# Modulation products of 512 columns in four column tiles, and a first layer that is modulated after its transpose

## What is computed

```python
h = rms_norm(x, g) * (1 + scale) + shift      # shift, scale, gate: rows of silu(cond) @ ada_w + ada_b
# cond = c_ctx for the 128 context tokens, c for the 256 latent tokens
aq, ak, av, bq, bk, bv, bo, bg = split(h @ ab_w_in)      # layer 0: attention and mLSTM
... mixers ...; x = x + gate * mixed; then a mixture of 32 experts; the same for layer 1
```

## Time and profile before

| | us |
|---|---|
| median of 3 runs | 1768.45 |
| lowest and highest | 1767.39, 1774.14 |
| span of the profiled execution | 1768.3 |
| TensorE busy | 1582.3 (89%) |
| VectorE busy | 427.1 (24%) |
| ScalarE busy | 301.4 (17%) |
| first product of TensorE | 16.8 |
| first product of the input projection | 58.7 |
| end of the last modulation chunk of the projection's rounds | 197.3 |

### The profile page before, as it was taken

How to read it: one execution, slowest core, us unless ns; L and a number is a source line. 1 busy time by engine, 2 the same in 40 slices (tenths; PEclk the granted TensorE clock), 3 DMA queues, 4 the chain that set the end, 5 groups by cost and what they waited for, 6 DMA issues and landing times.

```text
span 1768.3 us, 21532 instructions
## 1 busy us (share of the span) xinstructions
PE 1582.3 (89%) x8498; PEld 781.0 (44%) x8498; DVE 427.1 (24%) x911; ACT 301.4 (17%) x606; POOL 145.3 (8%) x199
## 2 busy tenths in 40 slices
PE   4899876897999999999957998898899999999991
PEld 3454775644443333334423445654333333344440
DVE  0212275423311111111113022323411111111113
ACT  1100112411111111111112003431111111111112
POOL 1101103000000000000014000010000000000000
PEclk8899977697999999999987998998899999999996
DMA  9977944024999999999969422022499999999982
GB/s 352 256 255 258 347 179 161 1 75 166 372 423 423 424 424 423 424 423 424 423 278 303 159 95 84 1 76 113 179 419 423 424 424 423 423 424 424 423 372 110
DMA packets 99382, 522.15 MB, mean 295 GB/s; under 512 B 10090, under 2 KB 11562, under 8 KB 56320
## 3 DMA queue, kind: packets, MB, share of 16 engines
q1 hardware_dynamic: 85920, 485.58, 68.1%
q0 software_dynamic: 13408, 35.81, 6.4%
HBM read 511.60 MB, written 20.22 MB: 301 GB/s over the span
## 4 chain that ended last, share of the span: by engine, by line
PE 82%; DVE 6%; DMA 6%; ACT 3%; issue 2%; SPq 1%; POOL 0%; DVEq 0%; POOLq 0%; ACTq 0%
PE psum L827 24%; PE psum L517 14%; PE psum L840 12%; PE psum L808 9%; PE psum L773 5%; DMA ring<-in_moe_w 3%; PE psum L833 2%; PE psum L814 2%; PE psum L820 2%; PE psum L460 2%; PE psum L726 2%; PE psum L688 1%; PE psum L706 1%; ACT area_g L1091 1%; DMA ring<-in_ada_w 1%
## 5 line engine op out<-in xcount | busy, mean ns | idle before, releaser
L827 PE MATMUL psum<-ring,area_t 128*64 128x512 f32 x1024 | 450.1, 592 | 3.5 <-DMA ring<-in_moe_w 1.4
L828 PE MATMUL psum<-ring,area_t 128*64 128x512 f32 x1024 | 450.4, 593 | 0.0
L827 PEld LDWEIGHTS psum<-ring,area_t 128*64 128x64 f32 x1024 | 139.3, 137 | 292.8 <-issue 291.3
L517 PE MATMUL psum<-ring,area_t 128*128 128x512 f32 (+1 forms) x576 | 241.6, 581 | 0.0
L840 PE MATMUL psum<-ring,area_t 128*64 128x512 f32 x1024 | 235.5, 602 | 2.2 <-DVE area_t L1676 2.2
L808 PE MATMUL psum<-area_h,area_t 128*64 128x512 f32 x768 | 180.0, 604 | 3.0 <-DVE area_t L1661 3.0
L1647 DVE COPY area_q<-psum 64x512 f32<-64x512 f32 x64 | 44.5, 695 | 570.6 <-PE psum L828 570.5
L517 PEld LDWEIGHTS psum<-ring,area_t 128*128 128x128 f32 x576 | 110.0, 192 | 127.6 <-issue 125.8
L1853 POOL DMA_INDIRECT pair_rows<-area_q,idx x64 | 62.3, 973 | 940.3 <-ACT area_q L1137 925.7
L828 PEld LDWEIGHTS psum<-ring,area_t 128*64 128x64 f32 x1024 | 139.3, 137 | 0.0
L840 PEld LDWEIGHTS psum<-ring,area_t 128*64 128x64 f32 x1024 | 68.7, 137 | 120.5 <-issue 113.1
(11 more groups left out here) (238 smaller groups left out, 1363.0 us busy)
## 6 DMA issues: line engine op xcount, KB each, us to landing
ring<-in_moe_w SPq DMA_DIRECT2D x192, 2048.0 KB, 16.2
ring<-in_ada_w SPq DMA_DIRECT2D x24, 2048.0 KB, 16.9
ring<-in_na_w_in SPq DMA_DIRECT2D x6, 2048.0 KB, 18.0
ring<-in_ab_w_in SPq DMA_DIRECT2D x5, 2048.0 KB, 11.3
area_m<-mod_ready POOLq DMA_DIRECT2D x6, 1024.0 KB, 8.9
area_q<-pair_rows POOLq DMA_DIRECT2D x6, 1024.0 KB, 7.0
ring<-in_ab_w_out SPq DMA_DIRECT2D x2, 2048.0 KB, 15.6
area_g<-mod_ready POOLq DMA_DIRECT2D x4, 1024.0 KB, 7.7
```

What stands on the lines that cost most here:

```text
L517: mm = pe.matmul(banks[2 + g % 4][:, 0:w], hT[:, k, t * P:t * P + P], wchunk(n, KT)[:, k, 0:w], start=(k == 0), stop=(k == KT - 1))
L827: pe.matmul(banks[2 + u][0:64, :], lhsT, w1[:, k, :], start=(k == 0), stop=(k == KT - 1))
L828: mm = pe.matmul(banks[2 + u][64:128, :], lhsT, w3[:, k, :], start=(k == 0), stop=(k == KT - 1))
```

## The change

- A modulation chunk is 8 products with 512 columns instead of 32 with 128. Product k goes to column tile k % 4; each tile sums two k, and PSUM bank 7 holds four partial sums of one chunk. Every chunk is copied by ScalarE for itself (24 copies instead of 6), and a chunk's first product waits for the copy of the chunk before it. In DRAM `mod_raw` has a dimension of 4 for the partial sums, which VectorE adds in `modulation` (three more additions for each group).
- In the projection's rounds from the second on, one of the two modulation chunks runs after the first token tile and one after the third (`ADA_AFTER`), instead of both at the end.
- For the first layer h is no longer made row by row. `turn_first` turns x while it scales: the moving operand is a diagonal matrix with the reciprocal norm (`first_diagonal`). When a chunk has been copied, `columns` sums the partial sums and turns them into columns by four products with two columns each; VectorE adds the bias columns and the gain, and `hT` is scaled and shifted by partition, by VectorE (six operations for each half) and ScalarE (two).
- The first input chunk is loaded third instead of fifth, and projected in two halves of k: the first four k when chunks 0 and 2 (shift and scale of the first 512 features) are through, the others after chunks 1 and 3. It uses three PSUM banks at once.
- GpSimd loads 24 rows of bias and gain instead of the bias row and the repeated gain row, no longer waits for h_ready ahead of the small loads, and SyncE no longer waits for first_gain_loaded. The stores and reads of groups are put in another order: group 4 is fetched ahead of the mLSTM state stores.

```diff
+        FIRST = [(0, 0), (0, 2), (0, 1), (0, 3)]
...
-        stream = [("ada", 0, c) for c in range(4)]
+        stream = [("ada",) + q for q in FIRST[0:2]] + [("in", 0, 0)] + [("ada",) + q for q in FIRST[2:4]]
...
                 for k in range(KT):
-                    for j in range(4):
-                        mm = pe.matmul(banks[7][32 * j:32 * j + 32, 128 * (c % 4):128 * (c % 4) + 128],
-                                       cond32[:, k, :], w[:, k, 128 * j:128 * j + 128],
-                                       start=(k == 0), stop=(k == KT - 1 and not (l == 0 and c < 4)),
-                                       skip_group_check=True)
...
+                    j = k % 4
+                    mm = pe.matmul(banks[7][32 * j:32 * j + 32, :], cond32[:, k, :], w[:, k, :],
+                                   start=(k < 4), stop=(k >= 4), skip_group_check=True)
...
+            def columns(l, c):
+
+                n = ADA_NUM[l, c]
+                if n == 0:
+                    pe.wait_ge(S["first_ready"], 1)
+                pe.wait_ge(S["ada_copied"], n + 1)
+                for i in range(4):
+                    col = (c // 2) * 2 * KT + 2 * (4 * (c % 2) + i)
+                    mm = pe.matmul(banks[6][:, col:col + 2], modsb[:, n % 2, P * i:P * i + P], keep[:, KEEP["cond"]],
+                                   start=True, stop=True)
+                mm.then_inc(S["cols_done"], 1)
...
+            def project_first():
+
+                n = NUM["in", 0, 0]
+                for half in range(2):
+                    for c in (half, half + 2):
+                        ada(0, c)
+                        columns(0, c)
+                    pe.wait_ge(landed[place(n)], when(n))
+                    pe.wait_ge(S["first_scaled"], 2 * half + 2)
+                    for t in range(NT):
+                        for k in range(4 * half, 4 * half + 4):
+                            mm = pe.matmul(banks[2 + t][:, :], hT[:, k, t * P:t * P + P], wchunk(n, KT)[:, k, :],
+                                           start=(k == 0), stop=(k == KT - 1), skip_group_check=True)
+                        if half:
+                            mm.then_inc(S["proj_done"], 1)
+                ada_step(("in", 0))
...
+            def first_columns(half):
+
+                v.wait_ge(S["cols_done"], 2 * half + 2)
...
+                v.wait_ge(S["trans_copied"], 2 * NT)
+                for k in range(4 * half, 4 * half + 4):
+                    for c, cols in enumerate((slice(0, P), slice(P, 3 * P))):
+                        if c == 0 or k % 4 >= 2:
+                            ins = v.tensor_scalar(hT[:, k, cols], hT[:, k, cols], scale0[:, k, c:c + 1],
+                                                  shift0[:, k, c:c + 1], ALU.mult, ALU.add)
...
-            get(first_gain, spread(a["norm_mix"][0]), "first_gain_loaded")
...
             get(early, a["early"], "early_loaded")
 
-            pool.wait_ge(S["h_ready"], NT)
             gv = a["ab_q_norm"][0]
             get(qkgain[:, 0:A_HEADS, :], gv.unsqueeze(0).unsqueeze(0).to_broadcast([P, A_HEADS, HD]), "small_loaded")
...
+            finish_mod(4)
             pool.wait_ge(S["cstate_ready"], 2)
```

More of the change, by code:

```diff
@@ L464, in ada @@
[L464 to L471, removed]
-                mm.then_inc(S["ada_done"], 1)
@@ L474, in ada_step @@
-            def ada_step(which):
-                for q in ADA_AT[which]:
-                    ada(*q)
[L478 to L490, removed]
+                    j = k % 4
@@ new lines, in turn_first @@
+            def turn_first(t):
+                pe.wait_ge(S["h_ready"], t + 1)
+                for half in range(2):
+                    n = 2 * t + half
+                    if n >= 2:
+                        pe.wait_ge(S["trans_copied"], n - 1)
+                    for k in range(4):
+                        d0 = (4 * half + k) * P
+                        mm = pe.matmul(banks[n % 2][:, k * P:k * P + P], x[:, t, d0:d0 + P], diag[:, t, :],
+                                       start=True, stop=True)
+                    mm.then_inc(S["trans_done"], 1)
@@ L492, in transpose_rows, with ada_step @@
+            def ada_step(which, part=None):
+                for q in ADA_AT[which] if part is None else ADA_AT[which][part:part + 1]:
+                    ada(*q)
             def transpose_rows(idx, t):
@@ L1184, in _ @@
                 squares(t)
-            ada_copy(0)
-            for c in range(2):
-                act.wait_ge(S["first_spread"], c + 1)
-                step(act.copy(spread_view(modB[:, c, :]), spread_banks(c, 0)), "first_B")
+            for t in range(NT):
+                copy_transposed(0, t)
+            for half in range(2):
+                ada_copy(0, half)
+                ada_copy(0, half + 2)
+                scale_first(half)
             for l in range(2):
-                for t in range(NT):
-                    copy_transposed(2 * l, t)
+                if l:
+                    for t in range(NT):
+                        copy_transposed(2 * l, t)
                 copy_projected(l)
@@ L1254, in modulation @@
                 v.wait_ge(S["cmod_loaded"], 32 * G)
-                m = cmod[:, G % 2, :, :, :]
+                m, r = cmod[:, G % 2, :, :, :], craw[:, G % 2, :, :]
+                flat = m.rearrange("p c v i -> p (c v i)")
+                tt(flat, r[:, 0, :], r[:, 1, :], ALU.add)
+                for j in range(2, 4):
+                    tt(flat, flat, r[:, j, :], ALU.add)
                 for c in range(2):
@@ L1751, in rows @@
                         normed(idx, t - behind)
-            first_modulation()
             for t in range(NT):
-                normed(0, t)
+                first_diagonal(t)
+            v.wait_ge(S["first_rows_turned"], 1)
+            cp(first.rearrange("p v k -> p (v k)"), banks[6][:, 32:32 + 3 * KT], "first_ready")
+            for half in range(2):
+                first_columns(half)
             for l in range(2):
```

171 lines of the change are left out of this document (101 added, 70 removed).

## The result

| | us |
|---|---|
| before, median of 18 runs | 1767.06 (1763.21 to 1774.14) |
| after, median of 18 runs | 1779.29 (1764.93 to 1783.32) |
| ratio after to before | 1.0052, 95% interval 1.0035 to 1.0069 |
| span of the profiled execution, before and after | 1768.3, 1777.7 |

The change makes the kernel slower, by 0.5% or 9 us: inside the range (1753 to 1785), and 4 us worse than the +4.9 of the forecast. It lies right at the bound of 0.5% between "no change" and "slower": the interval leaves out 1, and has values on both sides of 1.005.

A forecast was written before the change was run, and what follows sets the result against it. The start was taken to be bound by weight arrival, slowed by uncovered small loads, then by TensorE. Mark +3.3, rounds +1.0, turned pair +0.9, attention -0.3 gave +4.9 on 1768.3: 1773 us, range 1753 to 1785.

The forecast's parts named there:

- What bounds the start: Kernel start: uncovered small loads slow weight streaming for 23 us to 1.88 MB, so modulation chunk 2 arrives at 41 us.
- Rival A: Small loads at the start cost only their bytes, 1.9 us: mark at 72.5, whole 1757.6 us; chance 0.20.
- first half: First four k of the first input projection: 12 products, 10.4 us plus 1.8 for low clock, from 49.0 to 61.2.
- Rival B: Modulation chunks: four tiles with long products run two at a time, 3.47 us a chunk, +35, 1808 us; chance 0.05.
- rival C: First projection: clock stays low through the broken-up start, halves 20.8 us instead of 12.2, +17, 1790 us; chance 0.07.
- The mark: End of the first projection chunk and its two modulation chunks: 88.1 us instead of 84.79, +3.3.
- open stretch: Between the projection halves: two modulation products, copies, columns and VectorE with nothing to cover them, 10.4 us.
- second half: Remaining k of the first input projection: 12.2 us, from 71.6 to 83.8, with the same clock loss of 1.8.
- pair: Two modulation chunks after the first projection, with one copy between them: 1.8 + 0.7 + 1.8 = 4.3 us.
- Rounds: Five later projection rounds, modulation chunks standing apart and switching the tiling twice: +1.0 us, bounds -1 and +3.
- turned pair: Behind the projections: second turned chunk waits for ScalarE's copy of the first, 0 to 1.8 us, taken +0.9.
- Attention: End of the mLSTM: a pair adds 0.6, earlier group fetch lets the key copy start up to 0.8 sooner; net -0.3 us.

The follow-up runs named there:

- the first attempt: Changed kernel with GpSimd's small loads made to wait until two projection chunks are done, ahead of the modulation stores in its queue: ratio 1.0151 to the kernel before.
- the second: Changed kernel with the unslimmed small loads issued after the store of modulation chunk 7, so no store waits behind them: ratio 0.9960 to the kernel before.

## Why the prediction was right, and where it was off

**What bounds the start** held. The forecast put a slow stretch of 23 us with 1.88 MB of weights behind the removed wait. After has 2.45 MB from 17 to 41 us. Chunk 2 was foreseen for 41 and came at 41.91, and the wait ahead of it was 13.05 (I had said about 20, with TensorE's work ahead of it done by about 22; transposes, chunk 1 and its columns took until 28.9). That was the one step that decided the sign. Rival A, by which the loads cost only their bytes, asked for the first half near 33. It was near that (33.1 to 37.3) only in the kernels that take the loads or their packets away. Rival B fell with chunks of 1.85 to 1.92 us at the high clock (3.64 at the low one, for chunk 2), rival C with halves of 12.48 and 13.26.

The Trainium skill ("DMA: Bandwidth & Descriptors", Queues, rings and completion order) says that engines take turns between queues packet by packet. The trace agrees: 174 packets of q0 beside 170 of q1 in 14 us. It is less even with the two gain loads alone in the kernel before, 165 beside 253 in the same 14 us. In after a packet of q0 took 1.2 us of an engine and one of q1 0.079 x 14 x 16 / 170 = 0.10, so that equal turns were no equal shares.

**The mark** was sized at +3.3 and was +6.1. Step by step, against the forecast:

| step | forecast | after | difference |
|---|---|---|---|
| chunk 2's product begins | 41.0 | 41.91 | +0.9 |
| from there to the first half | 8.0 | 8.83 | +0.8 |
| first half | 12.2 | 12.48 | +0.3 |
| open stretch | 10.4 | 9.84 | -0.6 |
| second half | 12.2 | 13.27 | +1.1 |
| pair | 4.3 | 4.57 | +0.3 |

The largest is the second half. I gave the clock's loss, 1.8 us, to both halves alike; against 10.4 at the high clock the first lost 2.1 and the second 2.9. The dense first half did leave the clock high, as I took it to, for the open stretch. The windows of after (columns as above) show where it went:

```profile
63.00:71.00 8.00, 6.03 (x49) 2.77 (x48) 0.38 (x3) 1.17 (x2) 0.00 (x0) 1.00 0.98 363
71.00:73.00 2.00, 0.00 (x0) 0.00 (x0) 1.88 (x7) 1.09 (x2) 0.00 (x0) 0.68 0.48 185
73.00:77.00 4.00, 3.94 (x5) 1.85 (x6) 0.00 (x0) 0.00 (x0) 0.00 (x0) 0.50 0.07 27
77.00:79.00 2.00, 2.00 (x4) 0.78 (x3) 0.00 (x0) 0.00 (x0) 0.00 (x0) 0.61 0.00 0
79.00:87.00 8.00, 8.00 (x26) 3.20 (x28) 1.26 (x2) 0.58 (x1) 0.00 (x0) 1.00 0.00 0
```

The granted clock was 1.00 until 71 us, fell to the lower of its two levels (1.2 GHz) while TensorE had nothing to do (from 70.5 to 73.06), stayed there in the first 4 us of dense work and was back at the upper one (2.4 GHz) before 79.

The arrival of chunk 2 is the next, 0.9. Of the 0.8 behind it, 0.5 are the four products with two columns, 1.88 us at half clock where I took 1.4 between 0.9 and 1.8: the upper bound was the value. The other 0.3 are VectorE's, 2.6 where I took 2.3.

Two sums of the forecast are slightly off, and nothing hangs on them: the upper bound of the open chain adds up to 12.7, not 12.5, and the terms given for the upper end of the range to 1786.5, not 1785.

**Rounds and turned pair.** Rounds: foreseen +1.0, measured 113.96 - 112.58 = +1.4 for the five (90.90 to 204.86, before 84.79 to 197.37). A full round has 0.26 of it: 0.07 for two chunks at 1.85 us instead of 1.815, the rest for the projection in two pieces (7.06 + 13.93 = 20.99 instead of 20.80). Turned: foreseen +0.9, measured 0.36. The first row shows the 1.67 us for the copy that I had counted. But before, TensorE waited 1.84 us for VectorE at this place, and the delay falls into that wait. In after VectorE still comes last, by 0.39:

```profile
212.38 1.92 PE L459 MATMUL psum<-ring,cond 128*32 128x512 f32 x16 [1.67 <-ACT area_m L1011]
214.69 0.39 PE L561 MATMUL psum<-small,keep 128*128 128x4 f32 x2 [0.39 <-DVE small L1265]
```

**Attention** was foreseen at -0.3; from the sums to the turned keys it was -0.65 (83.91, before 84.56), and the 6.48 us wait of VectorE is gone. The size proves little: kernels with this part of after's code unchanged took 83.7 to 86.2 us for it.

**Behind that** the sum had nothing, and the trace has +3: attention itself +0.4, from there to the first expert product +1.3, and the rest +2.6 until the last expert product and -2.1 behind it. I didn't find one cause for these. The projection of layer 1 is one part, 125.63 instead of 124.17 us. The change doesn't touch it: all 24 modulation chunks are done by 295 us. The difference goes with the clock of these two executions, in the first 7 us (before, then after):

```profile
944.93:952.00 7.07, 7.07 (x17) 3.16 (x17) 0.00 (x0) 0.58 (x1) 7.07 (x11) 0.91 1.08 311
...
955.03:962.00 6.97, 6.97 (x13) 3.00 (x13) 0.00 (x0) 0.58 (x1) 6.97 (x11) 0.70 1.07 311
```

The last group of expert products is another: 5.35 us before and 3.65 in after, 1.7 of the -2.1. Together: 6.1 + 1.7 - 0.65 + 0.4 + 1.3 + 2.6 - 2.1 = 9.4, the difference of the spans. The medians differ by 12.2, the ratio by 9.

**The chances.** 0.63 was given to "within 0.5%", and the ratio lies at 1.0052, on the bound. Of the 4 us between the forecast and the ratio the mark has 2.8, by the terms of the table: the same mechanism, mostly with more of the low clock than I took. The rest lies behind the sums and is not assigned. That the spans of before and after differ by just the ratio's 9 us is in part luck: both traced executions had attention at its slow end (66.0 and 66.4 us), and one at the fast end would have moved the difference by 10.

## What to carry to other kernels

When a wait is removed, ask what was queued behind it and had been kept out of the way by it, and price such loads by their packets beside the streaming queue, not by their bytes. A row that is needed several times in a partition is loaded once and repeated by the engine that reads it. When a load is moved, look at both sides of its new place: here the first attempt stalled the stores behind it, and the second the weights beside it.

## What the runs showed of the hardware that was not expected

- A load of 256 KB that writes one row of 256 bytes 1024 times took 17.1 to 22.1 us to land in six kernels. With its neighbour of 256 rows alone moved to the front of the kernel before, the weight queue moved 0.52 MB in 14 us; in after, with the other small loads behind them, 0.35. Written 128 times it landed after 9.1 us, and q1 moved 7.21 MB in the 24 us where it moved 2.45.
- Moved to the front of the kernel before, these two loads cost 16 us at the mark, where the larger took 22.1 to land.
- A store of 16 KB took 22.3 us to land behind such loads in GpSimd's queue, and 6.3 ahead of them.
- Four column tiles with 512 columns overlap as well as with 128: 16 instructions of a chunk in 1.85 to 1.92 us, against 64 in 1.815. Fewer instructions saved nothing.
- Attention, with next to the same code and the same data, took 55.8 to 66.4 us in the traced executions of eleven kernels, with granted clocks of 0.88 to 0.65. The time ahead of it in the launch doesn't sort them: keys turned at 284 us had 57.7 and 55.8, at 278 and 281 us 66.3 and 65.9, and at 304 and 307 us 57.7 and 55.9.
